# The first four blocks of an adaLN conditioning product, summed wholly by TensorE

## The reference, cut to what matters

```python
c_act = jax.nn.silu(c)                      # c: (1, 1024)
mod = c_act @ ada_w[l] + ada_b[l]           # ada_w: (1024, 9 * 1024)
sh1, sc1, g1, sh2, sc2, g2, sh3, sc3, g3 = jnp.split(mod, N_MOD, axis=-1)
h = modulate(rms_norm(x, norm_ffn1[l]), sh1, sc1)          # x: (1, 512, 1024)
x = x + 0.5 * g1[:, None, :] * swiglu(h, ffn1_w_gate[l], ffn1_w_up[l], ffn1_w_down[l])
h = modulate(rms_norm(x, norm_mix[l]), sh2, sc2)
x = x + g2[:, None, :] * token_mixing(h, ...)
h = modulate(rms_norm(x, norm_ffn2[l]), sh3, sc3)
x = x + 0.5 * g3[:, None, :] * swiglu(h, ...)
return rms_norm(x, final_norm)
```

## Time and profile before

| | us |
|---|---|
| median of 3 runs | 1151.31 (1150.41 to 1154.48) |
| the profiled execution | 1150.95 |
| its span | 1148.9 |
| TensorE busy, of the span | 1131.1 (98%) |
| VectorE busy | 738.0 (64%) |
| ScalarE busy | 493.1 (43%) |
| GpSimd busy | 117.2 (10%) |
| mean granted clock of TensorE, of full speed | 0.998 |

### The profile page before, as it was taken

How to read it: one execution, slowest core, us unless ns; L and a number is a source line. 1 busy time by engine, 2 the same in 40 slices (tenths; PEclk the granted TensorE clock), 3 DMA queues, 4 the chain that set the end, 5 groups by cost and what they waited for, 6 DMA issues and landing times.

```text
span 1148.9 us, 17467 instructions
## 1 busy us (share of the span) xinstructions
PE 1131.1 (98%) x6378; PEld 988.0 (86%) x6378; DVE 738.0 (64%) x1167; ACT 493.1 (43%) x758; POOL 117.2 (10%) x115
## 2 busy tenths in 40 slices
PE   8899999999999999999999999999999999999997
PEld 7788888888888998888888888889899999988887
DVE  4766665666544666675555666757789899962332
ACT  5232332232222247655645656633445454542232
POOL 3301000000110001102002230000410110100000
PEclk9999999999999999999999999999999999999999
DMA  9567566557677425438236755242334545343331
GB/s 308 171 207 251 193 200 218 167 166 243 211 246 234 126 74 118 111 98 176 85 94 132 158 118 124 76 125 76 101 102 130 146 118 156 95 119 98 91 115 74
DMA packets 244174, 167.95 MB, mean 146 GB/s; under 512 B 6198, under 2 KB 224516, under 8 KB 244116
## 3 DMA queue, kind: packets, MB, share of 16 engines
q1 hardware_dynamic: 227188, 143.48, 41.8%
q0 software_dynamic: 16208, 21.33, 8.9%
q10 hardware_dynamic: 720, 2.36, 0.6%
HBM read 164.99 MB, written 16.05 MB: 158 GB/s over the span
## 4 chain that ended last, share of the span: by engine, by line
PE 90%; DVE 2%; SPq 2%; DMA 2%; issue 2%; ACT 1%; POOL 0%; DVEq 0%; POOLq 0%; ACTq 0%
PE bank L1909 28%; PE bank L1911 28%; PE bank L1910 28%; PE bank L2277 2%; PE bank L2270 1%; PE bank L2293 1%; SPq L604 1%; PE bank L2265 1%; PE bank L2292 1%; DMA raw<-in_ffn_w_gate_dram 1%; SPq L623 1%; DMA adas<-in_ada_w_dram 1%; SPq L617 1%; DVE hL L1298 0%; DVE tmp L1293 0%
## 5 line engine op out<-in xcount | busy, mean ns | idle before, releaser
L1909 PE MATMUL bank<-hH,wH 128*128 128x512 f32 (+1 forms) x976 | 355.3, 364 | 5.2 <-DVE hL L1298 3.3
L1911 PE MATMUL bank<-hH,wL 128*128 128x512 f32 (+1 forms) x976 | 351.2, 360 | 0.0
L1910 PE MATMUL bank<-hL,wH 128*128 128x512 f32 (+1 forms) x976 | 351.0, 360 | 0.0
L810 ACT ACTIVATE wH<-raw 128x1024 fp32r<-128x1024 f32 x131 | 135.8, 1037 | 350.6 <-PE bank L1911 348.0
L1232 DVE TENSOR_TENSOR wL<-raw,wH 128x1024 fp32r<-128x1024 f32 x131 | 156.6, 1195 | 200.5 <-ACT wH L810 199.7
L1909 PEld LDWEIGHTS bank<-hH,wH 128*128 128x128 f32 x976 | 184.1, 189 | 35.0 <-issue 5.3
L1911 PEld LDWEIGHTS bank<-hH,wL 128*128 128x128 f32 x976 | 184.0, 189 | 27.9
L1910 PEld LDWEIGHTS bank<-hL,wH 128*128 128x128 f32 x976 | 184.2, 189 | 26.4
L1909 PE MATMUL bank<-actH,wH 128*128 128x512 f32 (+1 forms) x316 | 120.7, 382 | 0.0
L1911 PE MATMUL bank<-actH,wL 128*128 128x512 f32 (+1 forms) x316 | 120.4, 381 | 0.0
L1910 PE MATMUL bank<-actL,wH 128*128 128x512 f32 (+1 forms) x316 | 120.4, 381 | 0.0
(11 more groups left out here) (276 smaller groups left out, 1928.3 us busy)
## 6 DMA issues: line engine op xcount, KB each, us to landing
adaw<-in_ada_w_dram SPq DMA_DIRECT2D x28, 1024.0 KB, 6.1
raw<-in_mix_w_in_dram SPq DMA_DIRECT2D x41, 512.0 KB, 3.9
raw<-in_ffn_w_down_dram SPq DMA_DIRECT2D x32, 512.0 KB, 4.0
raw<-in_ffn_w_gate_dram SPq DMA_DIRECT2D x25, 512.0 KB, 4.0
raw<-in_ffn_w_up_dram SPq DMA_DIRECT2D x25, 512.0 KB, 4.0
adas<-in_ada_w_dram SPq DMA_DIRECT2D x16, 512.0 KB, 8.0
raw<-in_ffn_w_down_dram SPq DMA_DIRECT2D x16, 384.0 KB, 4.2
wsum_d<-in_ffn_w_gate_dram POOLq DMA_DIRECT2D x8, 704.0 KB, 8.0
```

Source lines behind the costliest of these rows:

```text
L810: nc.scalar.activation(wH[s][:, :n * P], raw[s][:, :n * P], ACT.Copy).then_inc(hi_done, 1)
L1909: T.matmul(o, a[0], b[0], start=start, stop=False)
L1910: T.matmul(o, a[0], b[1], start=False, stop=False)
L1911: return T.matmul(o, a[1], b[0], start=False, stop=stop)
```

## The change

`ROWS_PE` becomes all eight rows of all four blocks. `first_parts(b)` now has 4 groups of columns by 8 rows, 32 products, waits for both halves of the block and signals `adas_sum` itself. `first_rows` on GpSimd and on VectorE, and `first_sums`, are gone. `first_columns` has one sum to add to the bias where it had two or three. In `first_units` the places of the products and of the dummies are new.

```diff
-    ROWS_P = (2, 2, 2, 2)
-    CHAINED = (2, 3)
-    ROWS_PE = ((6, 7), (7,), (7,), (6, 7))
-    SUMS = [(() if b in CHAINED else (0,)) + (1,) + ((2,) if rows else ()) for b, rows in enumerate(ROWS_PE)]
+    ROWS_PE = (tuple(range(DT)),) * ADA0
+    SUMS = [(2,)] * ADA0
...
                 if n == 0:
-                    for b in range(ADA0):
-                        first_rows(b)
...
                 diagonals(0, slice(0, TT))
-                first_rows(0, 4, ROWS_V[0])
...
-                    if b in (1, 2):
-                        first_rows(b, ROWS_P[b], ROWS_V[b])
...
-                    if b == 3:
-                        first_rows(3, ROWS_P[3], ROWS_V[3])
...
             mean_squares(0, slice(0, TT))
-            first_rows(0, ROWS_P[0], 4)
...
             def first_parts(b):
 
-                pe.wait_ge(adas_in[b][1], 32)
+                for q in range(2):
+                    pe.wait_ge(adas_in[b][q], 32)
                 for e in range(AC // P):
                     for k in ROWS_PE[b]:
-                        T.matmul(bank[:, B_ADA_START[b], 8 + e:9 + e], adas[:, b, k, e * P:(e + 1) * P], csilu[:, k:k + 1],
+                        ins = T.matmul(bank[:, B_ADA_START[b], 8 + e:9 + e], adas[:, b, k, e * P:(e + 1) * P], csilu[:, k:k + 1],
                                  start=k == ROWS_PE[b][0], stop=k == DT - 1)
+                ins.then_inc(adas_sum, 1)
...
-                dummies(20)
+                dummies(12)
                 tiles(0, 0)
+                tiles(1, 0)
                 first_parts(1)
-                tiles(1, 0)
-                dummies(8)
-                first_sums(1)
                 for u in range(2, N_FIRST):
                     tiles(u, 0)
-                tiles(0, 1)
-                tiles(1, 1)
+                for u in range(3):
+                    tiles(u, 1)
                 first_parts(2)
-                tiles(2, 1)
-                first_sums(2)
                 tiles(3, 1)
+                dummies(8, B_ADA_START[1])
+                tiles(0, 2)
                 first_parts(3)
-                for u in range(3):
+                for u in range(1, N_FIRST):
                     tiles(u, 2)
-                first_sums(3)
-                tiles(3, 2)
                 dummies(4, B_ADA_START[2])
...
             first_parts(0)
-            first_sums(0)
```

More of the change, by code:

```diff
@@ L99, in hybrid_block @@
     AC, AC2 = 512, 512
-    ROWS_P = (2, 2, 2, 2)
-    CHAINED = (2, 3)
-    ROWS_PE = ((6, 7), (7,), (7,), (6, 7))
-    ROWS_V = [DT - len(rows) for rows in ROWS_PE]
-    SUMS = [(() if b in CHAINED else (0,)) + (1,) + ((2,) if rows else ()) for b, rows in enumerate(ROWS_PE)]
-    STEPS_P = [sum(2 * r - 1 for r in ROWS_P[:b]) for b in range(ADA0 + 1)]
-    STEPS_V = [sum(v - r for r, v in zip(ROWS_P[:b], ROWS_V)) for b in range(ADA0 + 1)]
+    ROWS_PE = (tuple(range(DT)),) * ADA0
+    SUMS = [(2,)] * ADA0
     N_FIRST = 4
@@ L662, in _ @@
                                     pattern=[[-1, P]], channel_multiplier=1).then_inc(ident_made, 1)
[L664 to L673, removed]
             def relative_table():
@@ L1354, in first_prep @@
                 V.tensor_tensor(l[:, :], r[:, :], f32(h[:, :]), ALU.subtract).then_inc(lo_done, 1)
[L1356 to L1373, removed]
             def first_columns(b):
```

## The result

| | kernel before | changed kernel |
|---|---|---|
| median, us | 1152.89 (4 runs, 1150.41 to 1155.14) | 1182.57 (4 runs, 1178.90 to 1183.59) |
| ratio | | 1.0257, 95% interval 1.0237 to 1.0277 |
| span of the profiled execution | 1148.9 | 1177.2 |
| TensorE busy | 1131.1 (98%) | 1162.1 (99%) |
| mean granted clock | 0.998 | 0.983 |

What follows compares the result with a forecast made beforehand. TensorE, busy 98%, was taken to bound the kernel: 13.7 us of work at full clock, 4 of slower dense matmuls and 9.5 of slower products make 27, from 1151.3 to 1178 us; forecast band 1174 to 1182 (54%), range 1164 to 1184.

Steps and rivals of the forecast that it cites:

- TensorE sets the end, nothing wins a delay back: Whole kernel: TensorE is busy 98%; what the start loses the whole loses, with only 4 us of later waits.
- The price of a record, 0.107: Blocks of products on TensorE: each record takes 0.107 us at full clock, a block of 64 records 6.85 us.
- the sum at full clock, 13.7 us: Start up to the last pair of tiles: 160 more records, 17.1 us, less idle time, dummies and additions; 13.7 us later.
- The rival by which a long row of records goes closer together: Product blocks: records under 0.063 us each, so the kernel is not slower, at best 1146 us; chance 2%.
- The clock falls in each block: Four blocks of products: granted clock falls to 0.50 in or right behind each block.
- The rival with a full clock: Start: the clock stays full through the blocks, 13.7 us slower, 1165 us; chance 6%.
- Products slow down about twofold at the low clock, 9.5 us: Product blocks after the fall: records take 0.2 us, adding 2.4 us a block, 9.5 us for four.
- the rival by which the products don't mind: Product blocks: the clock falls but records stay at 0.107 us; 17.5 us slower, 1169 us; chance 25%.
- Dense matmuls at the low clock, 4 us: Behind the blocks: dense matmuls at about 0.53 speed, 1.6 us lost behind blocks 1 and 3, about 4 us together.
- The step that the clock returns after about 3.4 us of dense work: Behind each block: the clock returns only after about 3.4 us of dense work or dummies.
- The rival that had the clock low for longer: Behind blocks: one or two more 3.4 us stretches at half speed, 5 to 8 us over forecast, up to 1186; chance 13%.
- The fall comes about 3.5 us into a block, later behind dense work: Product blocks: clock falls about 3.5 us in, later after dense work; the other 30 records or so cost 0.1 us more each.

Runs made afterwards that it cites:

- 64 columns: Changed kernel with every product's moving operand widened from one column of csilu to 64 equal ones, first result column read; 1164.6 us, 1.0101 to the kernel before.
- Half of the rows at full clock: Changed kernel without rows 0 to 3 of each block and with products of 64 equal columns; 1151.3 us, 0.9996 to the kernel before.
- half of the rows: Changed kernel with the products of rows 0 to 3 of each block left out, one-column products kept; 1161.6 us, 1.0071 to the kernel before.

## Why the prediction was right, point by point

- **The whole.** 1178 were forecast and 1182.6 measured, 0.6 us above the forecast's own band (1174 to 1182) and inside the range of 1164 to 1184. Of the 4.6 us, 1.6 are the kernel before, whose median moved from 1151.3 to 1152.9, and 1.9 the start (28.9 for 27); the rest is within the spread of the executions.
- **TensorE sets the end, nothing wins a delay back.** Right. The last pair was entered 28.9 us later, the span is 28.3 us longer; so 0.6 us came back somewhere in the 1100 us behind it. Of the 2.4 us of waits on `hL` in the earlier trace rows the 1.3 at 54.33 belong to the start; the other 1.1 are there after the change too.
- **The price of a record, 0.107, and the sum at full clock, 13.7 us.** Right, and shown by itself: 13.8 us with 64 columns, at 0.110 a record. Last pair forecast at 68.0, entered there at 68.4. The rival by which a long row of records goes closer together (under 0.063) falls with it. Half of the rows at full clock was forecast by the same sum at 54 to 55 and came at 54.6.
- **The clock falls in each block.** Right, four times of four. The rival with a full clock falls.
- **Products slow down about twofold at the low clock, 9.5 us.** Right: 0.214 against 0.107 a record, 9.7 us by the comparison with 64 columns; the rival by which the products don't mind falls. That the sum agrees to 0.2 us is partly luck: 3 us were reckoned for a block with nothing dense ahead and 2.4 on average, and the comparison gives 4.0 for block 0 and 1.7, 1.8 and 2.2 for the others. The weight load of the dummies (98 to 152 ns) pointed the right way, and the product's own went from 192 to 333. The Trainium skill's "TensorE: Matmul & The Clock Gate" (§ LDWEIGHTS) has one value, columns by 1.2 GHz, 107 ns for 128 columns. That agrees with the 0.107 us between records at full clock and is half of the 0.214 at the low clock.
- **Dense matmuls at the low clock, 4 us.** Too low: 5.4, of which 2.6 behind block 3 where 1.6 were reckoned. The step that the clock returns after about 3.4 us of dense work failed. In the changed kernel 12 dense matmuls took about 0.43 us each behind block 3, 5.3 us, before it was back, and with half of the rows the low stretch was nearly 5 us of dense work behind each block. The rival that had the clock low for longer was partly true (its stretches lasted 6.8 to 13.7 us, the one before 3.4), but at 1.4 us and not 5 to 8.
- **The fall comes about 3.5 us into a block, later behind dense work.** Roughly: 2.7 us into block 0 and 5.2, 5.0 and 4.7 into the others. But that doesn't mean that a shorter block is spared: with half of the rows I expected, beside block 0's fall, one more at most. There were three more, each 2.4 to 2.6 us into a block, and that kernel took 8 us where 0 to 3 were expected.
- **Transfers, GpSimd's and VectorE's removed work price at nothing.** Right: in the changed kernel no product waits for `adas`, and VectorE waits for TensorE before every block's columns (7.3, 9.7, 14.0 and 11.0 us).

The chain to reckon with is short: 13.8 of more work, 9.7 of slower products, 5.4 of slower dense work, 28.9 together.

## What to carry to other kernels

When work is moved to the engine that sets the end, price it twice: by its time at full clock, and by what it does to the clock of what stands behind it. A matrix-vector product keeps TensorE busy in every column of a profile and still let its clock fall here, so busy share is not the thing to read, the granted clock is. If such products must stay, repeat the moving column: 64 equal columns cost 0.110 us a record instead of 0.107 here and kept the clock at 1.00 in both kernels that had them. Forty cost nothing more, in rows of at most 32 records; of the two kernels with them one profile shows 1.00 throughout the start and the other a fall at 43.4. And look first for the slowest of several makers: one row less for GpSimd and the sums one place earlier gained 1.8 us here (0.3 to 3.3), where taking all rows from it lost 30.

## What the runs showed of the hardware

- The clock of an engine that is busy without a gap can fall: all four blocks of products of one column ended at 0.50, and with 16 columns too. With 64 columns it stayed at 1.00 throughout the start. With 40, in rows of 8 to 32 records, no fall began in a row of them; one began 0.9 us behind one, over dense matmuls.
- A float32 record's price hardly hangs on its columns: 0.107 us at full clock with one or 40 columns, 0.110 with 64; with one column at half clock 0.214. That its weight load sets the price fits the load's own records (192 ns and 333) and isn't shown by itself.
- One bf16 dummy of 256 columns behind every four records added 0.04 us each time and didn't hold the clock. With six dense matmuls behind every 16 records no fall began in any of six such groups; it came in or behind rows of 32 records.
- Stretches at 0.50 lasted from 3.4 us (over dummies) to 13.7 (20.2 to 33.9 in the changed kernel: products, dummies, five dense matmuls), and in one execution 10.2 us over mostly dense work. What decides that stays open.
